# Idle-time matmuls of a ones matrix in the norms and routers of a two-block transformer kernel

## What is computed

```python
def rms_norm(x, g):
    xf = x.astype(jnp.float32)
    y = xf * lax.rsqrt(jnp.mean(xf * xf, axis=-1, keepdims=True) + EPS)
    return (y * g.astype(jnp.float32)).astype(x.dtype)

def first_block(...):
    h = rms_norm(x, mix_norm_g[l]);  proj = h @ w_in[l]
    ...
    x = x + jnp.concatenate([y_a, y_b], axis=-1) @ w_out[l]
    h = rms_norm(x, ffn_norm_g[l])
    x = x + hier_moe(h, router_group_w[l], router_expert_w[l], w_gate[l], w_up[l], w_down[l])
    return rms_norm(x, final_norm_g)

def moe_swiglu(h, w_router, w_gate, w_up, w_down):
    logits = (xt @ w_router).astype(jnp.float32)
    top_logits, top_idx = lax.top_k(logits, TOP_K)
    ...
```

## Time and profile before

| | |
|---|---|
| time, median of 3 runs | 2283.08 us (2282.94 to 2287.41) |
| the profiled execution, its time | 2288.95 us |
| its span, first to last instruction | 2287.0 us |
| PE busy | 2032.6 us, 89% |
| DVE, ACT, POOL busy | 604.3, 486.2, 226.7 us |
| moved from and to main memory | 653.04 MB |
| mean granted TensorE clock | 0.925 |

### The profile page before, as it was taken

How to read it: one execution, slowest core, us unless ns; L and a number is a source line. 1 busy time by engine, 2 the same in 40 slices (tenths; PEclk the granted TensorE clock), 3 DMA queues, 4 the chain that set the end, 5 groups by cost and what they waited for, 6 DMA issues and landing times. The chain is left out here.

```text
span 2287.0 us, 38522 instructions
## 1 busy us (share of the span) xinstructions
PE 2032.6 (89%) x16903; PEld 1283.9 (56%) x16903; DVE 604.3 (26%) x1029; ACT 486.2 (21%) x632; POOL 226.7 (10%) x97
## 2 busy tenths in 40 slices
PE   6889687877878898899979887999999999899998
PEld 6888543333444698799979874343343334233434
DVE  4762321111111553444467532010001001000101
ACT  3521121111112442343444411000000000000001
POOL 4530000000000451000145100000000000000000
PEclk8999588888888899999989998999999999999999
DMA  7321299999999431255642423999999999999991
GB/s 269 111 111 41 88 426 425 424 424 424 423 424 415 152 120 56 84 175 186 223 143 87 172 110 120 375 395 418 419 418 418 419 418 419 418 419 417 404 385 47
DMA packets 134332, 653.04 MB, mean 286 GB/s; under 512 B 9777, under 2 KB 32433, under 8 KB 88881
## 3 DMA queue, kind: packets, MB, share of 16 engines
q1 hardware_dynamic: 134192, 650.95, 71.5%
HBM read 649.86 MB, written 1.05 MB: 285 GB/s over the span
## 5 line engine op out<-in xcount | busy, mean ns | idle before, releaser
L1748 PE MATMUL psum<-ring,arena 128*32 128x384 f32 (+1 forms) x3584 | 369.1, 542 | 3.7 <-DMA ring<-in_moe_w_up 3.1
L557 POOL TENSOR_TENSOR ring_r<-ring,ring_r 128x1024 fp32r<-128x1024 f32 x88 | 214.8, 2452 | 1020.2 <-ACT ring_r L547 1020.1
L510 PE MATMUL psum<-ring_r 128*128 128x256 f32 x1056 | 300.7, 285 | 0.0
L1748 PEld LDWEIGHTS psum<-ring,arena 128*32 128x32 f32 x3584 | 114.5, 110 | 223.0 <-issue 212.8
L508 PE MATMUL psum<-ring_r 128*128 128x256 f32 x704 | 206.1, 293 | 14.8 <-POOL ring_r L557 9.2
L1810 PE MATMUL psum<-ring,arena 128*32 128x512 f32 x1600 | 200.2, 602 | 9.5 <-DMA ring<-in_moe_w_down 9.5
L510 PEld LDWEIGHTS psum<-ring_r 128*128 128x128 f32 x1056 | 204.5, 194 | 0.0
L509 PE MATMUL psum<-ring_r 128*128 128x256 f32 x704 | 201.8, 287 | 0.0
L1511 PE MATMUL psum<-ring,arena 128*32 128x512 f32 x1024 | 143.7, 714 | 19.3 <-DMA ring<-in_w_up 19.3
L1954 DVE TENSOR_TENSOR arena<-arena,psum 128x512 f32<-128x512 f32 (+1 forms) x42 | 23.7, 617 | 510.0 <-PE psum L1754 359.4
L508 PEld LDWEIGHTS psum<-ring_r 128*128 128x128 f32 x704 | 138.4, 197 | 17.1 <-issue 11.1
(11 more groups left out here) (375 smaller groups left out, 2712.9 us busy)
## 6 DMA issues: line engine op xcount, KB each, us to landing
ring<-in_w_gate SPq DMA_DIRECT2D x64, 1024.0 KB, 15.7
ring<-in_w_down SPq DMA_DIRECT2D x32, 2048.0 KB, 21.0
ring<-in_w_up SPq DMA_DIRECT2D x64, 1024.0 KB, 19.8
ring<-in_moe_w_gate SPq DMA_DIRECT2D x64, 1024.0 KB, 21.7
ring<-in_moe_w_down SPq DMA_DIRECT2D x64, 1024.0 KB, 21.2
ring<-in_moe_w_up SPq DMA_DIRECT2D x48, 1024.0 KB, 19.7
ring<-in_moe_w_gate SPq DMA_DIRECT2D x64, 768.0 KB, 21.5
ring<-in_moe_w_up SPq DMA_DIRECT2D x48, 768.0 KB, 21.8
```

The lines of the kernel that those rows point to most:

```text
L510: return nc.tensor.matmul(out, al, bh, start=False, stop=stop, **kw)
L557: nc.gpsimd.tensor_tensor(lo[:, :, c], w[:, :, c], w_hi[:, :, c].bitcast(F32), ALU.subtract)\
L1748: mm = nc.tensor.matmul(bank(b0 + j)[n * MORE:(n + 1) * MORE, 0:Q], z_Xg[:, x:x + MORE], w[:, (2 * h + j) * Q:(2 * h + j + 1) * Q], start= ...
```

## The change

A helper multiplies the ones matrix with itself into the first 128 columns of a bank that nobody reads before it is written anew. It is called 13 times, 262 matmuls in all, always directly in front of a wait of TensorE; `m.groups` is 4 in the first router and 0 in the second.

```diff
+        def keep_warm(b, n):
+
+            for _ in range(n):
+                nc.tensor.matmul(bank(b)[:, 0:P], ones[:, :], ones[:, :], start=True, stop=True)
+
@@ mixer1_tensor
             pe.wait_ge(*v.at("ready"))
+            keep_warm(5, 18)
             norm_tensor(pe, st, "n")
-
+            keep_warm(5, 44)
             pe.wait_ge(*v.at("h"))
@@ route_tensor
             norm_tensor(pe, st, "n")
+            keep_warm(6, 17)
             pe.wait_ge(*v.at("h"))
...
                     e.name(f"hrow{t}{half}")
 
+            keep_warm(5, 30 if m.groups else 8)
             pe.wait_ge(*v.at("chosen"))
...
             e.name("counted")
+            keep_warm(5, 12 if m.groups else 34)
@@ mixer2_tensor
             norm_tensor(pe, st, "f")
+            keep_warm(6, 14)
             norm_tensor(pe, st, "n")
+            keep_warm(6, 20)
             pe.wait_ge(*v.at("h"))
@@ hgrn_tensor
+            keep_warm(3, 8)
             norm_tensor(pe, st, "n", [V["ffn"].at("x")])
+            keep_warm(6, 20)
             pe.wait_ge(*v.at("h"))
```

## The result

| | before | after |
|---|---|---|
| median of 4 runs | 2283.05 us (2282.94 to 2287.41) | 2257.05 us (2255.99 to 2259.34) |
| profiled execution, its span | 2288.95, 2287.0 us | 2259.34, 2257.5 us |
| mean granted TensorE clock | 0.925 | 0.947 |

The ratio is 0.9883 with a 95% interval of 0.9866 to 0.9900: 26.0 us less, where 20 were forecast.

The account below looks back on a forecast made before the run. TensorE's pace or a VectorE and ScalarE chain bounds the kernel, weight transfers the two mixtures. Terms 3.3 + 6.3 + 0.4 + 1.5 + 3.2 + 5.1 = 19.8 us off 2288.95 give 2269.2, as median 2263; range 2252 to 2276.

Parts of the forecast that it names:

- Mixer 1: First norm to first projection: faster norm, part of L727's gain, some loss in the projection; 3.3 us, bounds 2.3 to 6.5.
- The run of 44: Added matmuls behind mixer 1's norm: 9.8 us, fitting in a 12.74 us pause and leaving 3 us of it.
- First router: Logits, transposes, counts and gather before the first mixture run faster; 6.3 us gained, bounds 1 and 10.5.
- Mixer 2: Second norm's gain lost to VectorE's wait for positions, leaving L2346; 0.4 us gained, bounds -0.5 and 1.8.
- Dense SwiGLU: Dense stage's projections lose their slow start at the lower clock level; 1.5 us gained, bounds 0 and 1.6.
- HGRN2: Its norm goes from 5.41 to 3.5 us and its projections' slow start is saved; 3.2 us, bounds 0 and 3.4.
- Second router: Logits and gather before the second mixture run at the upper level; 5.1 us gained, bounds 1 and 7.1.
- the clock that holds everywhere: Rival for all places: narrow matmuls never cost the upper level; 30.9 us gained, 2252, chance 0.12.
- The late runs: Rival: clock falls in narrow groups, later added runs partly overrun; about 9.5 us gained, 2274, chance 0.15.
- The transfers: Rival in the mixtures: loads run by their own clock and hide routers' and mixers' gains; 2283, chance 0.04.
- The slower case: Rival: added matmuls fail to raise the clock and most runs outlast their pauses; 39 us lost, 2322, chance 0.04.
- The rule weighed: Both routers: transposes would act as a pause for the clock; as a rival 4.7 us less gain, 2268, chance 0.05.

Follow-up runs that it names:

- pool_early: The kernel after, with GpSimd's wait for the constants moved behind its first weight remainders, so that it begins sooner; 2262.54 us, ratio 0.9909.
- pool_after_h: The kernel before, no added matmuls, with GpSimd held back until VectorE has written hT in mixer 1; 2277.62 us, ratio 0.9971.
- mix1_18: The kernel after, with only the 18 added matmuls before mixer 1's norm kept; 2274.70 us, ratio 0.9953.
- rest_only: The kernel after, without mixer 1's two runs of added matmuls; 2265.13 us, ratio 0.9919.
- routers_only: The kernel after, with only the two routers' runs of added matmuls kept; 2269.93 us, ratio 0.9936.
- mix1_only: The kernel after, with only mixer 1's two runs of added matmuls, 18 and 44, kept; 2275.65 us, ratio 0.9964.
- narrow_fill: The kernel after, with all added matmuls 8 moving columns wide in place of 128; 2299.21 us, ratio 1.0070.
- loop_fill: The kernel after, with ten more added matmuls before spread_back in each of the first mixture's iterations; 2252.71 us, ratio 0.9858.

## Why the prediction was right, and where it was off

The direction and the range held, 2257 against 2263, within 2252 to 2276, and outside mixer 1 the mechanism did too. But some 6 us of the 26 came by a mechanism that the prediction did not have, VectorE freed from GpSimd; in pool_early, where this is taken away, the change gave 21.2 us, near the 20 forecast. By its steps:

- **Mixer 1**, forecast 3.3 with bounds 2.3 to 6.5, measured 9.3 at the projection. This is the mis-sized term, and it lies outside its bounds. The norm's part was right (6.58 to 3.72). The step that failed is "It moves forward whole, since VectorE's L491, which ends it, starts earlier by the same 3.1": the pause of 12.74 us was taken as a chain of fixed length, though 11.6 of it were eight operations that need 3.3. pool_after_h shows that holding GpSimd back is enough, pool_early that with GpSimd beside it the term comes out at 3.0. The trace of before held the evidence: minimum 474 ns, median 1520 for the same operation, and GpSimd's group over the same stretch. I had read the group's sum only.
- **The run of 44** was forecast to be covered; it ends 5 us late and keeps L733 fast in return. By mix1_18 both together are worth nothing.
- **First router**, 6.3 forecast, measured 7.1 to the first gate and up, 8.3 to the first load. The logits' clock fell in their middle (5.25 us, 3.6 forecast) and the transposes weren't halved, but `spread_back` and the first gate and up gave more than the 0.5 taken for them: the stretch from L1503's start to L1520's is 12.4 us, 16.6 before. Where the level held, the part up to the gate and up gave more: 8.9 us in rest_only, 9.6 in routers_only.
- **Mixer 2**, 0.4 forecast: the lead goes from 17.2 at the first load to 17.5 at the dense projection, 0.3. The positions hold VectorE up as said. L2357, behind a pause of 4.83 us, is slower than before, 6.40 us against 5.31, but not through the 20: the same group took 5.31 to 6.22 us in the kernels without added matmuls there and 4.92 to 6.58 in those with wide ones.
- **Dense SwiGLU**, 1.5 forecast: 17.5 to 19.1, so 1.6. **HGRN2**, 3.2 forecast: 19.1 to 21.8, so 2.8, its norm in 3.72 us (3.5 forecast) where it took 5.41. That this term came out is in part luck. pool_after_h has no added matmul and has the fast norm too, as have mix1_only and mix1_18:

```profile
1133.58 3.72 PE L481 MATMUL psum<-arena,ones 128*128 128x256 f32 x16 [2.57 <-DVE xT L2720]
```

In these three the dense stage is 1.1 us longer in return. Only both stages together tell the gain: from the first dense projection to the second router's norm it is 407.5 to 408.0 us in the six kernels without added matmuls there (before among them) and 403.0 to 404.3 in the seven with wide ones. So they give 3.2 to 5.0 us, where 4.7 were forecast, but nothing shows that the 8 in front of the norm bring 1.9 of it.
- **Second router**, 5.1 forecast: 21.8 to 27.6 at the gate and up, 5.7. Logits and gather 3.74 and 3.78 as forecast; the transposes were slow.
- **Second mixture**, not in the sum: another 2.1 us by the last norm. It is hardly the change's: from its first gate and up to the last norm before's profiled execution took 877.8 us and after's 875.7, but pool_after_h and mix1_only, without an added matmul from the first router on, took 876.0 and 875.9, and all kernels lie between 873.5 and 877.8. So before's profiled execution was a long one here.

At the last norm the lead is 29.7 us, 9.9 more than the sum of 19.8. Mixer 1 has 5.6 of that (8.9 at the first router's norm against 3.3), the other places 2.2 (27.6 less 8.9, against 16.5), the second mixture 2.1, most of it no effect of the change. The medians show 3.6 less than the profiled pair, since before's profiled execution lay 5.9 above its median and after's 2.3.

Of the rivals, the clock that holds everywhere didn't come: it fell in both routers. The late runs came in mixer 1 only, the 44. The transfers hid nothing. The slower case needs narrow added matmuls (narrow_fill, 2299; priced at 2322 for wide ones that fail).

The rule weighed, that transposes don't count for the clock, stands in the Trainium skill, "TensorE: Matmul & The Clock Gate", Part 4 (PE-mode transpose). After's second router speaks against it, as the earlier trace rows did: the transposes run at 0.50, and behind them, from 1354.3 to 1356 us, the clock is 1.00. But the prediction read only one of the two routers of before. In the first, the same 16 transposes (241.48, 3.65 us) were followed by 0.50:

```profile
245.20:247.20 2.00, 0.00 (x0) 0.00 (x0) 1.06 (x6) 0.67 (x2) 0.00 (x0) 0.50 0.00 0
```

So transposes can bring the level back and need not. What took it away in the second router was the narrow group in front of them, not they: behind wide logits they keep 1.00.

What stays open: why a narrow group loses the level in one execution and keeps it in another, with the same work in front. In the first router the same program did both, in after (logits at 225.76) and in loop_fill (227.53). The runs show that it happens, not the condition; each kernel was profiled once. So counts alone forecast such a change to a few us and no better.

## What to carry to other kernels

Filling TensorE's waits with wide matmuls pays where the group behind the wait is on the path. The fill must be wide (8 columns made this kernel slower), and it should end before the signal, so size it by the wait that is left after the change. Before a pause is taken as fixed, compare the minimum and the median of the operation that ends it, and look at what VectorE and GpSimd do side by side: here their order alone was worth 6.1 us, with no added matmul. Where transfers bound a stage, only what precedes its first load counts.

## What the runs showed of the hardware

- VectorE's 128x256 operation with two inputs in on-chip memory took 0.48 us alone and 2.56 beside a GpSimd operation of 2.52 us: one of VectorE's passed per one of GpSimd's. The Trainium skill, "SBUF — State Buffer", section "SBUF: two separate sides", states the rule: such a VectorE instruction and a GpSimd instruction that reads that memory share a port pair, which whoever starts first holds for the whole instruction. The trace agrees, in steps of 2.5 us. It also goes the other way, to a degree: in after, GpSimd's four took 11.64 us where they took 9.96 before, while VectorE's L538 ran beside them.
- From 8 to 128 columns width is nearly free here: 16 f32 matmuls of 8 columns took 3.74 us at the upper level, of 128 columns 3.84.
- TensorE busy in 16.0 of 16 us almost all with 8 to 32 columns (narrow_fill, 246 to 262 us), stayed at 0.50, and a narrow group could lose 1.00 without a pause (225.8 to 231 us in after).
